# One core of a hybrid mLSTM / sparse-attention / mixture-of-experts block: overflow rows in blocks of 32 instead of 128

## The reference

```python
def hier_moe(h, wg, bg, we, be, w1, w3, w2):
    hf = h.reshape(T, D)                                  # T = 1024 tokens, D = 1024
    p_grp = softmax(hf @ wg + bg)                         # 4 groups, the best one
    le = (hf @ we + be).reshape(T, 4, 8)                  # 8 experts in each group
    p_in = softmax(le[arange(T), grp])                    # the best 2 of the group
    gate = pg_top * pe_top / sum(pe_top)
    ...
    return grouped_expert_ffn(hf, eidx, gate, w1, w3, w2)

# for every token and each of its two experts e (32 experts):
#   y += gate * ((silu(x @ w1[e]) * (x @ w3[e])) @ w2[e])
# w1, w3: 1024 x 512, w2: 512 x 1024, all float32
```

## Time and profile before

| | us |
|---|---|
| median of 3 runs | 1542.26 (1536.59 to 1545.73) |
| the profiled execution's own time | 1540.23 |
| its span, first to last instruction | 1537.9 |
| PE busy | 1348.6 (88%) |
| DVE busy | 599.2 (39%) |
| ACT busy | 397.1 (26%) |
| granted TensorE clock, mean | 0.949 of full |

### The profile page before, as it was taken

One profiled execution on the slowest core, in us unless ns is written; L12 is line 12 of the kernel. 1 busy time (PEld: TensorE's weight loads), 2 busy tenths in 40 slices (PEclk: granted clock), 3 DMA queues, 4 the chain that ended last, 5 costly groups with the idle time before them and its releaser, 6 DMA issues.

```text
span 1537.9 us, 17232 instructions
## 1 busy us (share of the span) xinstructions
PE 1348.6 (88%) x6333; PEld 678.6 (44%) x6333; DVE 599.2 (39%) x1325; ACT 397.1 (26%) x878; POOL 82.4 (5%) x114
## 2 busy tenths in 40 slices
PE   5999999999996889988899946999999899899750
PEld 3644444454664445444455533444434343344320
DVE  3536456310344766666423353222322232223206
ACT  4243311114665555555122210000000000000005
POOL 0000000010003000000000001000000000000004
PEclk9999999999997999999999967999999999999985
DMA  9713136130005960000452264999999999999939
GB/s 339 161 41 127 61 140 219 55 110 0 1 1 139 260 209 1 1 1 0 186 198 82 96 259 159 397 401 406 393 399 405 414 400 404 398 403 409 400 118 302
DMA packets 109451, 326.67 MB, mean 212 GB/s; under 512 B 26797, under 2 KB 51001, under 8 KB 100793
## 3 DMA queue, kind: packets, MB, share of 16 engines
q1 hardware_dynamic: 96296, 295.67, 51.3%
q0 software_dynamic: 6288, 18.90, 3.9%
q10 hardware_dynamic: 6784, 11.02, 2.0%
HBM read 285.69 MB, written 42.49 MB: 213 GB/s over the span
## 4 chain that ended last, share of the span: by engine, by line
PE 31%; SPq 14%; DMA 6%; DVE 5%; issue 3%; ACT 2%; POOL 1%; ACTq 0%; DVEq 0%; POOLq 0%
SPq L657 11%; PE ps L1478 7%; PE ps L1520 6%; DMA arena<-expert_w 5%; PE ps L1570 4%; PE ps L1531 4%; PE ps L1379 2%; PE ps L1396 2%; PE ps L1416 2%; SPq L655 1%; SPq L705 1%; ACT arena L1045 1%; POOL arena L847 1%; PE ps L1510 1%; PE ps L1458 1%
## 5 line engine op out<-in xcount | busy, mean ns | idle before, releaser
L1232 PE MATMUL ps<-arena 128*128 128x512 f32 x512 | 222.0, 593 | 0.0
L1531 PE MATMUL ps<-arena 128*32 128x256 f32 (+1 forms) x1408 | 194.7, 492 | 27.5 <-DMA arena<-expert_w 25.2
L1570 PE MATMUL ps<-arena 128*32 128x256 f32 (+2 forms) x832 | 154.4, 500 | 4.3 <-issue 2.4
L1232 PEld LDWEIGHTS ps<-arena 128*128 128x128 f32 x512 | 96.6, 190 | 117.8 <-issue 117.7
L1243 PE MATMUL ps<-arena 128*128 128x512 f32 (+1 forms) x384 | 144.8, 535 | 1.4 <-DVE arena L1666 1.4
L1531 PEld LDWEIGHTS ps<-arena 128*32 128x32 f32 (+1 forms) x1408 | 73.8, 125 | 134.5 <-issue 116.9
L1520 PE MATMUL ps<-arena 128*128 128x512 f32 x256 | 115.8, 611 | 5.9 <-DVE arena L2087 5.9
L1478 PE MATMUL ps<-arena 128*128 128x512 f32 x256 | 112.7, 592 | 0.1
L1045 ACT ACTIVATE arena<-arena 128x640 f32<-128x640 f32 (+7 forms) x128 | 92.7, 726 | 59.5 <-DVE arena L1879 59.5
L1243 PEld LDWEIGHTS ps<-arena 128*128 128x128 f32 x384 | 72.8, 192 | 66.5 <-issue 57.3
L1396 PE MATMUL ps<-arena 128*128 128x128 f32 x528 | 79.8, 284 | 21.4 <-ACT arena L1045 9.2
(11 more groups left out here) (333 smaller groups left out, 1282.1 us busy)
## 6 DMA issues: line engine op xcount, KB each, us to landing
arena<-expert_w SPq DMA_DIRECT2D x99, 2048.0 KB, 34.7
arena<-ada_w SPq DMA_DIRECT2D x12, 2048.0 KB, 9.2
d_y<-arena SPq DMA_DIRECT2D x24, 512.0 KB, 6.1
arena<-x SPq DMA_DIRECT2D x16, 512.0 KB, 4.2
arena<-w_in SPq DMA_DIRECT2D x4, 2048.0 KB, 10.9
d_y<-arena ACTq DMA_DIRECT2D x40, 128.0 KB, 8.2
arena<-w_out SPq DMA_DIRECT2D x2, 2048.0 KB, 14.1
out<-arena SPq DMA_DIRECT2D x8, 512.0 KB, 3.7
```

Of the source, the lines that this page charges most:

```text
L1232: last = nc.tensor.matmul(b, w(k), hT[:, k, 512 * c:512 * c + 512], start=(k == 0), stop=(k == KT - 1))
L1531: last = nc.tensor.matmul(ps[width * j:width * j + width, 2 if width == 64 else 3, 0:span], xgT[s][:, k, lo:lo + width], w_up[slots[n]][:, ...
L1570: last = nc.tensor.matmul(dst, hid_T[s][:, at_:at_ + width], w_down[slot][:, k, span * j:span * j + span], start=(k == 0), stop=(k == 3))
```

## The change

- An overflow block has 32 rows, and runs as the 32-row places do, in four column groups (`rows = 32` in `f_turn`, `f_up`, `f_turn_hidden`, `f_down`, `gated`, `hidden`, `result`). Each block still loads its expert's three weight blocks.
- Blocks needed per expert: rows over its room, divided by 32 and rounded up (before: by 128).
- The loop on each engine has 4 rounds with 24 nested `If`s, so up to 96 blocks. `PER = 24` replaces `NOV = 24`. Before the body held two blocks, now it holds 24.
- The number of blocks is `n_over`, in all lanes. The expert of each block is computed with one lane per block (`block_expert`, 96 lanes) and brought into one row (`block_tab`) through DRAM: SP stores it to `d_expert` ahead of the first weight load that waits for the table, and reads it back ahead of the 50th load.
- `gather_over` also waits until the gather of the block before has landed. The index column is copied from lanes 32*(s mod 4) on.
- ACT stores a block by four transfers of 32 x 256.

The diff, cut to its core:

```diff
@@ -699,7 +699,11 @@
             load_static(8)
             sp.wait_ge(stage_end["E"], 4)
             sp.wait_ge(table_ready, 1)
+            sp.dma_start(d_expert, block_expert[0:4 * PER, :]).then_inc(table_in, 16)
             for v in range(NS - 1, len(LOADS)):
+                if v == 50:
+                    sp.wait_ge(table_in, 16)
+                    sp.dma_start(block_tab, d_expert.rearrange("p a -> a p")).then_inc(table_in, 16)
                 n, q = LOADS[v]
                 place = ORDER[q]
                 e = sp.value_load(expert_at[place:place + 1, 0:1], min_val=0, max_val=NE - 1)
@@ -709,23 +713,24 @@
 
             def load_over(i, s):
 
-                e = sp.value_load(block_tab[0:1, bass.ds(2 * i + s, 1)], min_val=0, max_val=NE - 1)
-                sp.wait_ge(down_done, 2 * i + NE - 3 + s)
+                q = PER * i + NE + s
+                e = sp.value_load(block_tab[0:1, bass.ds(PER * i + s, 1)], min_val=0, max_val=NE - 1)
+                sp.wait_ge(down_done, q - 3)
                 sp.sem_inc(idx_seen, 1)
-                sp.wait_ge(up_done, 2 * i + NE - 1 + s)
+                sp.wait_ge(up_done, q - 1)
                 sp.sem_inc(idx_seen, 1)
-                load_weight(OVER_SLOT[s][0], 1, e)
-                load_weight(OVER_SLOT[s][1], 3, e)
-                sp.wait_ge(down_done, 2 * i + NE - 1 + s)
+                load_weight(OVER_SLOT[s % 2][0], 1, e)
+                load_weight(OVER_SLOT[s % 2][1], 3, e)
+                sp.wait_ge(down_done, q - 1)
                 sp.sem_inc(idx_seen, 1)
-                load_weight(OVER_SLOT[s][2], 2, e)
-
-            sp_blocks = sp.value_load(block_tab[0:1, 28:29], min_val=NE, max_val=NB)
-            with sp.Fori(0, (NB - NE) // 2) as i:
-                with sp.If(2 * i + NE < sp_blocks):
-                    load_over(i, 0)
-                    with sp.If(2 * i + NE + 1 < sp_blocks):
-                        load_over(i, 1)
+                load_weight(OVER_SLOT[s % 2][2], 2, e)
+
+            sp.wait_ge(table_in, 32)
+            sp_over = sp.value_load(n_over[0:1, :], min_val=0, max_val=4 * PER)
+            with sp.Fori(0, 4) as i, ExitStack() as rest:
+                for s in range(PER):
+                    rest.enter_context(sp.If(PER * i + s < sp_over))
+                    load_over(i, s)
             sp.wait_ge(up_done, NE)
             sp.dma_start(x2_back, d_x2.rearrange("(t p) n -> p t n", p=P)).then_inc(x2_in, 16)
             for t in range(NACC, NT):
...
             def gather_over(i, s):
 
-                pool.wait_ge(xg_turned, 2 * i + NE - 1 + s)
-                nc.gpsimd.tensor_copy(idx_col[s], row_tok[:, bass.ds(2 * i + NE + s, 1)]).then_inc(idx_ready[s], 1)
-                pool.wait_ge(idx_ready[s], i + 1)
+                lanes = slice(32 * (s % 4), 32 * (s % 4) + 32)
+                pool.wait_ge(xg_turned, PER * i + NE - 1 + s)
                 pool.sem_inc(idx_seen, 1)
-                pool.indirect_dma_start(xg[s], None, d_xn,
-                                        bass.IndirectOffsetOnAxis(ap=idx_col[s], axis=0),
-                                        bounds_check=S - 1, oob_is_err=False).then_inc(xg_in[s], 16)
+                pool.wait_ge(xg_in[(s + 1) % 2], 16 * (PER // 2 * i + (s + 1) // 2 + NE // 2))
+                nc.gpsimd.tensor_copy(idx_col[s % 2][0:32, :], row_tok[lanes, bass.ds(PER // 4 * i + NE + s // 4, 1)])\
+                    .then_inc(idx_ready[s % 2], 1)
+                pool.wait_ge(idx_ready[s % 2], PER // 2 * i + s // 2 + 1)
+                pool.sem_inc(idx_seen, 1)
+                pool.indirect_dma_start(xg[s % 2][0:32, :], None, d_xn,
+                                        bass.IndirectOffsetOnAxis(ap=idx_col[s % 2][0:32, :], axis=0),
+                                        bounds_check=S - 1, oob_is_err=False).then_inc(xg_in[s % 2], 16)
 
             pool.wait_ge(table_ready, 1)
-            p_blocks = pool.value_load(block_tab[0:1, 28:29], min_val=NE, max_val=NB)
-            with pool.Fori(0, (NB - NE) // 2) as i:
-                with pool.If(2 * i + NE < p_blocks):
-                    gather_over(i, 0)
-                    with pool.If(2 * i + NE + 1 < p_blocks):
-                        gather_over(i, 1)
+            p_over = pool.value_load(n_over[0:1, :], min_val=0, max_val=4 * PER)
+            with pool.Fori(0, 4) as i, ExitStack() as rest:
+                for s in range(PER):
+                    rest.enter_context(pool.If(PER * i + s < p_over))
+                    gather_over(i, s)
             pool.drain().then_inc(stage_f, 1)
             pool.wait_ge(stage_f, 4)
...
             store(NE - 1, 1, STEP_ROWS[NE - 1], ORDER[NE - 1])
 
+            def over_block(i, s):
+
+                q = PER * i + NE + s
+                gated(q, s % 2, 32)
+                act.wait_ge(yo_ready, q + 1)
+                act.sem_inc(store_seen, 1)
+                to = d_y[bass.ds(32 * PER * i + P * NE + 32 * s, 32), :]
+                for n in range(4):
+                    act.dma_start(to[:, 256 * n:256 * n + 256], yo[s % 2][32 * n:32 * n + 32, 512:768]).then_inc(y_stored[s % 2], 16)
+
             act.wait_ge(table_ready, 1)
-            a_blocks = act.value_load(block_tab[0:1, 28:29], min_val=NE, max_val=NB)
-            with act.Fori(0, (NB - NE) // 2) as i:
-                with act.If(2 * i + NE < a_blocks):
-                    gated(2 * i + NE, 0, P)
-                    store(2 * i + NE, 0, P, 2 * i + NE)
-                    with act.If(2 * i + NE + 1 < a_blocks):
-                        gated(2 * i + NE + 1, 1, P)
-                        store(2 * i + NE + 1, 1, P, 2 * i + NE + 1)
-
-            act.wait_ge(y_stored[0], 32 * ((a_blocks + 1) // 2) + STORES[NE] - 16 * NE)
+            a_over = act.value_load(n_over[0:1, :], min_val=0, max_val=4 * PER)
+            with act.Fori(0, 4) as i, ExitStack() as rest:
+                for s in range(PER):
+                    rest.enter_context(act.If(PER * i + s < a_over))
+                    over_block(i, s)
+
+            act.wait_ge(y_stored[0], 64 * ((a_over + 1) // 2) + STORES[NE])
             act.sem_inc(store_seen, 1)
-            act.wait_ge(y_stored[1], 32 * (a_blocks // 2) + STORES[NE + 1] - 16 * NE)
+            act.wait_ge(y_stored[1], 64 * (a_over // 2) + STORES[NE + 1])
             act.sem_inc(store_seen, 1)
             act.drain().then_inc(stage_f, 1)
...
             def over_block(i, s):
 
-                q, slots = 2 * i + NE + s, OVER_SLOT[s]
-                loaded = [16 * i + 16 + n for n in OVER_FILLS[s]]
-                f_turn(q, s, P, i + NE // 2 + 1)
-                f_up(q, s, P, slots[0:2], loaded[0:2])
-                f_turn_hidden(q, s, P)
-                f_down(q, s, P, slots[2], loaded[2])
+                q, slots, nth = PER * i + NE + s, OVER_SLOT[s % 2], PER // 2 * i + s // 2
+                loaded = [16 * nth + 16 + n for n in OVER_FILLS[s % 2]]
+                f_turn(q, s % 2, 32, nth + NE // 2 + 1, over=True)
+                f_up(q, s % 2, 32, slots[0:2], loaded[0:2])
+                f_turn_hidden(q, s % 2, 32, over=True)
+                f_down(q, s % 2, 32, slots[2], loaded[2])
 
             pe.wait_ge(table_ready, 1)
-            e_blocks = pe.value_load(block_tab[0:1, 28:29], min_val=NE, max_val=NB)
-            with pe.Fori(0, (NB - NE) // 2) as i:
-                with pe.If(2 * i + NE < e_blocks):
-                    over_block(i, 0)
-                    with pe.If(2 * i + NE + 1 < e_blocks):
-                        over_block(i, 1)
+            e_over = pe.value_load(n_over[0:1, :], min_val=0, max_val=4 * PER)
+            with pe.Fori(0, 4) as i, ExitStack() as rest:
+                for s in range(PER):
+                    rest.enter_context(pe.If(PER * i + s < e_over))
+                    over_block(i, s)
             pe.drain().then_inc(stage_f, 1)
...
             link(V.tensor_tensor(excess, total_, cap, ALU.subtract))
-            link(V.tensor_scalar(over_i, excess, 0.0, float(P - 1), ALU.max, ALU.add))
-            link(V.tensor_single_scalar(over_i, over_i, 7, ALU.logical_shift_right))
-            link(V.tensor_copy(over, over_i))
+            link(V.tensor_scalar(over_i, excess, 0.0, 31.0, ALU.max, ALU.add))
+            link(V.tensor_single_scalar(over_i, over_i, 5, ALU.logical_shift_right))
+            V.tensor_copy(over, over_i)
+            link(V.tensor_scalar(base, place, float(P), None, ALU.mult))
             link(V.tensor_tensor_scan(over_inc, ones32, over, 0.0, ALU.mult, ALU.add))
             link(V.tensor_tensor(jump, over_inc, over, ALU.subtract))
-            link(V.scalar_tensor_tensor(jump, jump, float(NE), place, ALU.add, ALU.subtract))
-            V.scalar_tensor_tensor(jump, jump, float(P), cap, ALU.mult, ALU.subtract)
-            link(V.tensor_scalar(base, place, float(P), None, ALU.mult))
+            link(V.scalar_tensor_tensor(jump, jump, 32.0, base, ALU.mult, ALU.subtract))
```

(32 more changed lines are left out.)

25 lines of the change are left out of this document (7 added, 18 removed).

## The result

The changed kernel takes 1585.41 us (median of 4 runs, 1582.33 to 1586.1), the kernel before beside it 1543.99: a ratio of 1.0273, 95% interval 1.0234 to 1.0312. The prediction was 1590, in a range of 1572 to 1605. The profiled execution took 1586.07 us, its span is 1584.1, that is 46.2 more than 1537.9.

| piece | before | after | difference | predicted |
|---|---|---|---|---|
| start to first gather of rows | 930.5 | 933.3 | +2.7 | 0 |
| first gather to PE's first transposes | 5.3 | 9.4 | +4.1 | 0 |
| from there to the end of the last static place | 518.7 | 519.4 | +0.7 | 0 |
| from there to the end of the last overflow copy | 32.4 | 67.4 | +35.0 | +35.4 |
| that copy to the first gather of results | 7.5 | 11.2 | +3.8 | +13.9 |

A forecast was written before the change was run, and what follows sets the result against it. The prediction took PE to bound the present overflow block and the weight stream the four smaller ones; 32.2 + 3.2 + 13.9 = +49.3 on 1540.2 gave 1589.5, forecast as 1590, range 1572 to 1605.

The forecast's parts named there:

- The number of blocks: Overflow: one expert has about 117 rows beyond its room, so 4 blocks, loading 12 weight blocks where 3 were loaded.
- The stream of weights: Overflow blocks: nine more loads of 5.22 us queue, so the last block's copy ends later, +32.2 us.
- The rival of the dry queue: Overflow blocks: weights issued too late, the last two blocks each wait a load's whole way; 1604, chance 0.09 with similar losses.
- The clock: Last overflow block: its products run partly at TensorE's lower clock after waits for weights, +3.2 us, bounds 0 and 5.6.
- The table: Behind stage E: fewer DVE operations, one small SP store and its read back; taken as 0 us.
- Leaving the loop: Last copy to first gather of results: seven long jumps on ACT fetch code at 2.3 us each, +13.9 us.
- the bound of 4.5: Loop exit: higher price in us for each code fetch, from a 96 KB read, making the exit +29.3.
- code kept once it is fetched: Loop exit rival: one jump stalls or none, so the exit costs 0 to 2 us; 1575.6, chance 0.28.

The follow-up runs named there:

- the run with no reload: Changed kernel with only the first overflow block loading weights, the others using the same three slots: 1568.74 us, ratio 1.0163.
- The run with 64 rows: Changed kernel with overflow blocks of 64 rows in two column groups, 4 rounds of 12 nested blocks: 1558.84 us, ratio 1.0098.
- The one-round run: Changed kernel with overflow loops of 1 round of 24 nested blocks instead of 4 rounds: 1579.73 us, ratio 1.0240.
- the short body: Changed kernel with 24 rounds of 4 nested blocks instead of 4 rounds of 24: 1590.95 us, ratio 1.0313.
- with the store: Kernel before plus a store of 96 lanes x 4 bytes to DRAM ahead of the first weight load that waits for the table: 1542.15 us, ratio 0.9995.
- with four rounds: Kernel before with its loop over 128-row overflow blocks in 4 rounds of 6 nested blocks instead of 12 of 2: 1541.18 us, ratio 0.9987.

## Why the prediction was right, and where it was not

**The number of blocks** was read from the 0.48 MB of one gather and was right: 108 loads.

**The stream of weights** (+32.2 with the compute of the last block) was right, and the run with no reload shows it as the cause. The run with 64 rows fits it only in part, as its second block no longer waited for weights. From the end of the last static place to the end of the last copy it was to be 67.9 us with the clock's 3.2 (1454.5 to 1522.4), and is 67.4. The rival of the dry queue is out: the DMA share was 1.01.

**The clock** was taken as +3.2 for the last block. Its stretch from the first up product to the copy's end is 10.6 us, where the steps at full clock make 8.0: +2.6.

**The table** was priced at 0, between -2.6 and +0.4. This step failed. It looked at SP's time to issue the small store, and at what waited for the table, and not at what the store's own transfer does to the others on the DMA engines. The runs showed some 5 us in which all transfers together move 43 to 62 GB/s, wherever that store's writes met other transfers (three places of the store out of four); in the changed kernel this costs 4.1 us of the first gather, and moving the store behind the first weight load took 3.9 off the time from the first gather to the end.

**Leaving the loop** was mis-sized, at +13.9 where +3.8 was measured: seven stalls of 2.3 us, 16.1, were forecast on ACT. There were two, of 3.3 and 3.0, and beside them PE had one of 3.7 and DVE one of 2.6 (from its last copy, 1529.5, to its loop count, 1532.1). The stall was real and dearer than the 2.3 taken from small reads the earlier trace rows, within the bound of 4.5. What was wrong is that each far jump would pay it. The one-round run (one stall left, 6.7 us) and the short body (none) fix the count. The prediction's rival, code kept once it is fetched, had the kind of behaviour right and its number, one stall, too low: the way back was a second one. The rule that the prediction cited (the Trainium skill, Runtime: NRT & Kernel Launch, "Instruction fetch mechanics": a taken branch out of the two pages at hand forces a fetch) agrees with the first stall. As the prediction read it there would have been six more, and the trace has one, so here the measurement decides: what was fetched stayed for the later rounds. On PE even the first way back, to a head that it had left four blocks earlier, did not stall.

**The 2.7 us before stage F** lie within the spread between executions. The kernels whose code is that of before up to there issued the first gather at 929.1 (with the store) and 935.3 (with four rounds), against 930.5, and the versions of the changed kernel between 930.1 and 934.0.

So the total was right to 0.3% by luck in part: 10 us too much for the loop's end met 7 us that were not foreseen.

## What to carry to other kernels

Where weights stream at the DMA limit, a smaller block of rows is paid in whole sets of weights: count the loads, not the columns. Read how full the present block is from the bytes of its gather before halving it. And price a store like this one, 96 pieces of 4 bytes, by what lies under it on the DMA engines, not by its issue: place it where nothing waits for a transfer for the next 5 us. Behind a large load on the same queue its writes went out only after that load.

## What was not expected of the hardware

- After a store of 96 x 4 bytes from 96 partitions to DRAM all transfers of the core together ran at 43 to 62 GB/s for about 5 us, against 282 to 434 in stretches without it, with the DMA engines reading 62 to 90% busy. Issued behind a weight load, the same store left that load at full speed (347 GB/s), as its writes went out after it.
- A first jump over 20 blocks of code stalled ACT for 3.3 us and PE for 3.7 (4.6 in the one-round kernel), and later jumps to the same places took 0.2. Over 10 blocks of the 64-row kernel ACT did not stall (0.6 us).
- The same 64 products of 256 columns took 3.66 us when a block came every 10.2 us (granted clock 1.00), and 5.4 to 6.3 when it came every 15 to 16 (0.83).
